# The differential loop: value products in two halves, and part of the join on GpSimd

## The chip, the cores and the metric

The program runs on one core of a Trainium2 chip. The time is the device time of one execution in microseconds (us). Three timed runs of the kernel before gave 3054.6 us as the median (3054.22 to 3056.43).

## The reference, cut to what matters

The whole program is a two-layer transformer block followed by a second two-layer block (the lines `for l in range(L)` of the second half). The change lies in one branch of the second block, the differential attention, which is computed once in each of its two layers:

```python
def diff_attend(q1, q2, k1, k2, v, lam):
    s1 = jnp.einsum('bqhd,bkhd->bhqk', q1, k1) * scale
    s2 = jnp.einsum('bqhd,bkhd->bhqk', q2, k2) * scale
    p = jax.nn.softmax(s1, axis=-1) - lam * jax.nn.softmax(s2, axis=-1)
    return jnp.einsum('bhqk,bkhd->bqhd', p, v)
```

There are 4 heads, 512 latent queries and 256 context queries. A latent query sees 768 keys (512 latent, then 256 context). A context query sees the 256 context keys and is computed in layer 0 only. After it, `diff_post` normalizes each head's 64 values and scales them.

## The kernel before, in words

Every engine has its own program, written out in order by hand (`block.tensor`, `block.vector`, `block.scalar`, `block.gpsimd`, `block.sync`). They meet in semaphores: `done(key)` marks a step, `after(key)` waits for it.

A *unit* is 128 queries of one head. `df_units(l)` lists them: for each pair of heads `j` 8 latent units (`"d"`, 4 query blocks by 2 heads), and in layer 0 then 4 context units (`"dc"`). That is 24 units in layer 0 and 16 in layer 1, 32 of them latent. The loop makes one turn `i` per unit, and each engine does in turn `i`:

- TensorE: the first score of unit `i` (`df_score`, half 0, two matmuls into a pair of PSUM banks), the transposes of the joined weights of unit `i-2` (`turn_wide`, six of 128x128; `DF_LAG` is 2), the second score of unit `i`. In every second turn it then does the value products of a pair of units, the two heads (`values`, 12 matmuls in the program, 24 in the trace), and at a head pair's end a broadcast of the row sums (`shares`).
- VectorE: the row maximum of the first score (`df_top`, line 2990), the join of unit `i-1` (`df_join`: a reciprocal on line 2996, a 128x1 product that is the factor, and a 768-column `p = q * factor + p`), the row maximum of the second score.
- ScalarE: exp of the first score, the copy of the transposed weights of unit `i-2` out of PSUM (`df_down`), exp of the second score. An exp with a row sum is an ACTIVATE and an ACTIVATION_READ_ACCUMULATOR.
- GpSimd: nothing in the loop.

What holds the turns together are rings. `PB` is six PSUM banks, taken in pairs for the scores and the transposes, or singly. `PO` is two more banks for the value sums. `PR` has four slots for the exp results, two per unit, so the first exp of unit `i+2` waits until the transposes of unit `i` have read their slot. `PT` has three slots for transposed weights, and `ST` six for the factors.

At fixed turns (`df_post_at`) the loop also normalizes the finished outputs of a head pair. ScalarE squares them, TensorE averages them into a bank (`df_norm`, a bank of `PB`), ScalarE takes a root from it (`df_root`), VectorE refines it (`df_post`, which frees the bank, then `df_gain`). Behind the loop stands the last group of the output projection, which needs the last normalized outputs (`branch_low`).

In the names of the rows below, `banks` is PSUM, `arena` the working memory, `block_tokens_low` and `block_tokens_high` hold the keys and queries of the differential loop, and `mats` the identity that transposes. Line 850 is the helper of every matmul, 851 of every transpose, 1670 of every ScalarE activation and 2348 of every VectorE scalar_tensor_tensor.

Of the kernel before, what the change touches and what calls it, by code (L numbers as in the profile page):

```python
# [31 lines left out]
P = 128  # L32
D = 1024
KD = D // P
T = 512
TB = T // P
# [250 lines left out]
def build(nc, A, known):  # L287

    ctx = ExitStack()
    with ctx:  # L290
# [359 lines left out]
        for l in range(L):  # L650
# [36 lines left out]
            b["STAGE"] = [nc.dram_tensor(f"df_stage{l}_{j}", (4, P, T + CT), F32, kind="Internal").ap() for j in range(2)]  # L687
            b["KS"], b["QS"] = [[S[:, 4 * j:4 * j + 4, :] for j in range(2)] for S in (com["HT"], HI)]
# [39 lines left out]
        def df_post_at(l):  # L728

            n = len(df_units(l))  # L730
            return {(0, 0): n // 2 + (2 if l == 0 else 5), (0, 1): n // 2 + 5, (1, 0): n if l == 0 else None}
# [59 lines left out]
        def _(eng):  # L791
# [158 lines left out]
            def values(us, S, V, blocks, okey, first, last, q):  # L950

                if first:
                    PO.take(okey)
                    if PO.former:
                        eng.wait_ge(*after(PO.former))
                o = PO.get(okey)
                for u in us:
                    for part in range(0, blocks, 4) if u[0] not in ("d", "dc") else (0,):
                        eng.wait_ge(*after(("pt", u, part)))
# [5 lines left out]
                i.then_inc(*done(*[turned(S, u).free(u) for u in us], *((("out", okey),) if last else ())))  # L965
# [377 lines left out]
            for l in range(L):  # L1343
# [210 lines left out]
                def df_norm(j, side):  # L1554
                    norm_sums((("od", "odc")[side], l, j), S, range(1), 1, "head64", (T, CT)[side], PB)
# [10 lines left out]
                out_proj(1, range(2 - both, KD))  # L1566
                us = df_units(l)
                for i in range(len(us) + DF_LAG + 1):
# [11 lines left out]
                    if DF_LAG < i and us[i - DF_LAG - 1][4] == 1:  # L1580
                        u = us[i - DF_LAG - 1]
                        values([u[:4] + (h,) for h in range(2)], S,
                               lambda u, c: S["V"][:, c + (TB if u[0] == "dc" else 0), 64 * (2 * u[2] + u[4]):64 * (2 * u[2] + u[4]) + 64],
                               6 if u[0] == "d" else 2, df_okey(u), u[3] == 0, df_ends(u), u[3])
                        if df_ends(u):
                            shares(df_okey(u), S, u[3] + 1, 2)
# [80 lines left out]
        def _(eng):  # L1667
# [364 lines left out]
            for l in range(L):  # L2032
# [213 lines left out]
                def df_root(j, i):  # L2246
                    root((("od", "odc")[i], l, j), S, PB, (T, CT)[i])
# [11 lines left out]
                for i in range(len(us) + DF_LAG + 1):  # L2259
# [18 lines left out]
                    if DF_LAG < i and df_ends(us[i - DF_LAG - 1]):  # L2278
                        u = us[i - DF_LAG - 1]
# [65 lines left out]
        def _(eng):  # L2345
# [434 lines left out]
            for l in range(L):  # L2780
# [211 lines left out]
                def df_join(u):  # L2992
# [5 lines left out]
                    stt(s[:, 4:5], s[:, 3:4], S["RS"].get(df_okey(u))[:, at:at + 1], LAM[l][:, 4:5], MUL, MUL).then_inc(*done())  # L2998
                    eng.wait_ge(vector_step, done.count)
                    p, q = S["PR"].get((u, 0))[:, 0:n], S["PR"].get((u, 1))[:, 0:n]  # L3000
                    stt(p, q, s[:, 4:5], p, MUL, ADD).then_inc(*done(("p", u), S["ST"].free(u), S["PR"].free((u, 1))))

                def df_post(j, i):
# [6 lines left out]
                    stt(n, PB.get(("ms", tag))[:, 0:(T, CT)[i]], EPS, n, ADD, MUL).then_inc(*done(PB.free(("ms", tag)), ("stepped", tag)))  # L3010
# [23 lines left out]
                for i in range(len(us) + DF_LAG + 2):  # L3034
# [18 lines left out]
                    if DF_LAG + 1 < i and df_ends(us[i - DF_LAG - 2]):  # L3053
# [287 lines left out]
```

## Time and profile before

| | |
|---|---|
| median of three runs | 3054.6 us |
| the profiled execution's own time | 3056.31 us |
| its span | 3054.5 us |
| TensorE busy | 2844.1 us (93%) |
| VectorE busy | 1419.5 us (46%) |
| ScalarE busy | 1126.6 us (37%) |
| GpSimd busy | 237.3 us (8%) |
| differential loop of layer 0 | about 1646 to 1742 us of the span |
| differential loop of layer 1 | about 2583 to 2654 us of the span |

Busy shares are averages over the whole program, and the loop is about 5% of it. What bounds the loop is read from its own stretch. In a row of the timeline the first number is the start in us from the span's start, the second the time from the start of the first to the end of the last instruction of the row, and what stands in brackets is how long the engine was idle before it and what ended the idle time. The granted TensorE clock is given as a share of full speed.

### The profile page before, as it was taken

Reading aid. Unit: us, or ns where it says so; the run is one execution under the profiler, and the core shown is the slowest. Engines: PE = TensorE matmul, PEld = TensorE weight load, DVE = VectorE, ACT = ScalarE, POOL = GpSimd, SP = SyncE. Lnnn points to the kernel's source line nnn. Section 1 sums busy time; section 2 is a strip of 40 time slices with the busy share of each in tenths; the row PEclk is TensorE's granted clock in tenths of the full one; section 3 lists DMA queues with packets and bytes.
Section 4 is the critical chain, followed back from the end, with each engine's and each line's share of the span. In section 5 each row is a group of like instructions: output and inputs, shape, how many; then the busy total and the mean of one; then the engine's idle time right before and its main releaser. Section 6 shows DMA issues by size and latency. Waiting matters only on the chain.

```text
span 3054.5 us, 40084 instructions
## 1 busy us (share of the span) xinstructions
PE 2844.1 (93%) x16210; PEld 2104.2 (69%) x16210; DVE 1419.5 (46%) x2142; ACT 1126.6 (37%) x1913; POOL 237.3 (8%) x230
## 2 busy tenths in 40 slices
PE   7999979989999799999998789999999999689998
PEld 5657845447668655457787578888888787578886
DVE  6665432246665522245436653333235544643444
ACT  4665421134654411143244542222222432543332
POOL 1011010000111200010011010000002011000001
PEclk9999989999999899999999789999999999899999
DMA  4012249971012379964426112332221234222220
GB/s 154 29 42 73 95 192 419 415 308 63 15 42 100 123 329 416 418 263 154 150 75 166 42 42 111 123 126 111 111 83 44 91 101 140 68 74 98 98 98 33
DMA packets 68198, 430.37 MB, mean 141 GB/s; under 512 B 8001, under 2 KB 8385, under 8 KB 20401
## 3 DMA queue, kind: packets, MB, share of 16 engines
q1 hardware_dynamic: 62432, 410.05, 35.2%
q0 software_dynamic: 4432, 15.67, 1.6%
q8 instruction: 131, 2.15, 0.3%
q10 hardware_dynamic: 1152, 2.10, 0.2%
q14 instruction: 51, 0.41, 0.0%
HBM read 418.87 MB, written 8.91 MB: 140 GB/s over the span
## 4 chain that ended last, share of the span: by engine, by line
PE 80%; DVE 7%; DMA 5%; ACT 4%; issue 2%; POOL 2%; SPq 0%; DVEq 0%; ACTq 0%; POOLq 0%
PE banks L850 76%; PE banks L851 3%; DMA weight<-in_w_up 3%; ACT arena L1670 3%; DVE arena L2348 3%; POOL arena L3145 1%; DVE arena L2990 1%; DVE weight_part L2452 1%; DMA weight<-in_w_in 1%; DMA weight<-in_ada_w 1%; ACT weight_part L1670 0%; DVE arena L2637 0%; DMA block_tokens_high<-df_stage 0%; DVE arena L2635 0%; DMA arena<-na_stage 0%
## 5 line engine op out<-in xcount | busy, mean ns | idle before, releaser
L1670 ACT ACTIVATE arena<-banks 128x512 f32<-128x512 f32 (+3 forms) x506 | 277.6, 551 | 892.0 <-PE banks L850 788.5
L850 PE MATMUL banks<-weight,arena 128*64 128x512 f32 (+4 forms) x2136 | 443.0, 581 | 21.4 <-DMA weight<-in_w_up 9.3
L850 PE MATMUL banks<-hidden,weight_part 128*128 128x512 f32 (+1 forms) x2304 | 446.8, 355 | 0.0
L850 PEld LDWEIGHTS banks<-hidden,weight_part 128*128 128x128 f32 x2304 | 381.1, 189 | 70.4 <-issue 3.8
L850 PE MATMUL banks<-tokens_high,weight_part 128*128 128x512 f32 (+1 forms) x1536 | 412.7, 360 | 8.7 <-ACT tokens_high L1670 5.5
L2452 DVE TENSOR_TENSOR weight_part<-weight,weight_part 128x2048 fp32r<-128x2048 f32 x124 | 285.8, 2308 | 191.6 <-ACT weight_part L1670 191.5
L1670 ACT ACTIVATE weight_part<-weight 128x2048 fp32r<-128x2048 f32 x124 | 236.4, 1908 | 372.9 <-PE banks L850 344.9
L850 PEld LDWEIGHTS banks<-weight,arena 128*64 128x64 f32 (+2 forms) x2136 | 150.8, 136 | 268.0 <-issue 246.3
L850 PEld LDWEIGHTS banks<-tokens_high,weight_part 128*128 128x128 f32 x1536 | 276.3, 192 | 62.8 <-DVE arena L2348 12.1
L3145 POOL TENSOR_TENSOR arena<-arena 128x512 f32<-128x512 f32 (+1 forms) x90 | 117.1, 1301 | 1999.1 <-ACT arena L1670 1732.3
L850 PE MATMUL banks<-tokens_low,weight_part 128*128 128x512 f32 (+1 forms) x768 | 265.4, 355 | 0.0
L850 PE MATMUL banks<-arena 128*64 128x128 f32 (+3 forms) x2048 | 223.7, 315 | 12.4 <-DMA arena<-na_stage 5.3
L2348 DVE SCALAR_TENSOR_TENSOR x<-banks,arena,x 128x512 f32<-128x512 f32 x192 | 142.4, 749 | 183.4 <-PE banks L850 182.7
L1670 ACT ACTIVATE arena<-banks,arena 128x512 f32<-128x512 f32 (+2 forms) x264 | 182.1, 694 | 90.7 <-DVE arena L2990 57.0
L851 PE MATMUL banks<-mats,arena 128*128 128x128 f32 (+1 forms) x1112 | 171.6, 289 | 39.4 <-DVE arena L2640 20.6
L3095 DVE TENSOR_TENSOR hidden<-arena,hidden 128x768 fp32r<-128x768 f32 (+1 forms) x64 | 52.8, 826 | 315.4 <-ACT hidden L1670 315.4
L851 PEld LDWEIGHTS banks<-mats,arena 128*128 128x128 f32 (+1 forms) x1112 | 131.6, 147 | 93.9 <-issue 45.0
L850 PEld LDWEIGHTS banks<-arena 128*64 128x64 f32 (+2 forms) x2048 | 148.2, 153 | 61.4 <-issue 41.5
L850 PE MATMUL banks<-block_tokens_high,weight_part 128*128 128x512 f32 (+1 forms) x640 | 165.1, 353 | 2.6 <-ACT block_tokens_high L1670 2.6
L2348 DVE SCALAR_TENSOR_TENSOR arena<-arena 128x256 f32<-128x256 f32 (+5 forms) x225 | 120.1, 545 | 97.9 <-ACT arena L1670 91.5
L2399 DVE TENSOR_REDUCE arena<-banks 128x1 f32<-128x512 f32 (+1 forms) x160 | 97.8, 634 | 131.7 <-PE banks L850 129.3
L850 PEld LDWEIGHTS banks<-tokens_low,weight_part 128*128 128x128 f32 x768 | 144.9, 190 | 20.4
(214 smaller groups left out, 3889.6 us busy)
## 6 DMA issues: line engine op xcount, KB each, us to landing
weight<-in_w_gate SPq DMA_DIRECT2D x64, 1024.0 KB, 13.6
weight<-in_w_up SPq DMA_DIRECT2D x64, 1024.0 KB, 8.0
weight<-in_w_down SPq DMA_DIRECT2D x64, 1024.0 KB, 11.1
weight<-in_w_ff SPq DMA_DIRECT2D x64, 1024.0 KB, 4.8
weight<-in_ada_w SPq DMA_DIRECT2D x48, 1024.0 KB, 6.3
weight<-in_w_in SPq DMA_DIRECT2D x28, 1024.0 KB, 5.3
weight<-in_w_o SPq DMA_DIRECT2D x8, 1024.0 KB, 4.8
weight<-in_w_mem_kv SPq DMA_DIRECT2D x8, 1024.0 KB, 5.0
```

The source lines that it names most:

```text
L850: mm = lambda o, a, b, first=True, last=True: eng.matmul(o, a, b, start=first, stop=last, skip_group_check=True)
L851: tr = lambda o, a, rows=P: eng.transpose(o, a, mat("ident", rows, rows))
L1670: act = lambda o, i, f=ACT.Copy, **k: eng.activation(o, i, f, **k)
L2348: stt = lambda o, a, s, b, p, q: eng.scalar_tensor_tensor(out=o, in0=a, scalar=s, in1=b, op0=p, op1=q)
L2399: eng.tensor_reduce(s[:, 0:1], PB.get(("S", u))[:, 0:n], AX, MAX, negate=True).then_inc(*done(("nb", u)))
L2452: tt(low, raw_of(key), high, SUB).then_inc(*done(("split", key)))
L2990: eng.tensor_reduce(s[:, half:half + 1], PB.get_pair(key)[:, 0:T + CT if u[0] == "d" else CT], AX, MAX, negate=True).then_inc(*done(("nb", ...
L3095: tt(hid[:, 4 + m, 0:N], t[:, 0:N], hid[:, m, 0:N], SUB).then_inc(*done(("hid", l, s, m), S["RT"].free((l, s, m))))
L3145: eng.tensor_tensor(a, a, squares_of(tag, S).get((tag, k))[:, 0:n], ADD).then_inc(*done(squares_of(tag, S).free((tag, k)), *((("summed", t ...
```

## The change

It does four things.

1. The value products of a latent pair of units are issued in two halves of three key blocks each. The first half stands where all of it stood (behind the second score of turn `i`), the second half in the next turn between the first score and the transposes. The broadcast of the row sums moves with the second half. Context units keep theirs in one piece.
2. The join of a latent unit is split by columns. VectorE does columns 0 to 511, and GpSimd does the 256 context columns in two instructions: `q = q * factor` (a broadcast of one column), and `p = p + q`, which also waits for VectorE's part. The transposes wait for GpSimd's (`"pc"`).
3. In layer 1 the bank of the head average is taken from `PO` in place of `PB` (`MS`).
4. The normalization turns move: layer 0's first from turn 14 to 15 and its last from 24 to 25, layer 1's first from 13 to 14. The loops have one turn more.

```diff
+            b["MS"] = PB if l == 0 else PO
...
-            return {(0, 0): n // 2 + (2 if l == 0 else 5), (0, 1): n // 2 + 5, (1, 0): n if l == 0 else None}
+            return {(0, 0): n // 2 + (3 if l == 0 else 6), (0, 1): n // 2 + (5 if l == 0 else 6), (1, 0): n + 1 if l == 0 else None}
+
+        def df_ended(l, i):
+
+            us = df_units(l)
+            return [u for u in (us[n] for n in (i - DF_LAG - 1, i - DF_LAG - 2) if 0 <= n < len(us)) if df_ends(u) and us.index(u) == i - DF_LAG - (2 if u[0] == "d" else 1)]
...
-            def values(us, S, V, blocks, okey, first, last, q):
+            def values(us, S, V, blocks, okey, first, last, q, part=None):
+
+                cs = range(blocks) if part is None else part
...
-                for c in range(blocks):
+                for c in cs:
                     for h, u in enumerate(us):
                         i = mm(o[rows * h:rows * h + rows, q * P:(q + 1) * P], V(u, c), turned(S, u).get(u)[:, c, :], c == 0, c == blocks - 1)
...
                     if i < len(us):
                         df_score(us[i], 0)
+                    if DF_LAG + 1 < i and us[i - DF_LAG - 2][4] == 1 and us[i - DF_LAG - 2][0] == "d":
+                        df_values(us[i - DF_LAG - 2], range(3, 6))
                     if DF_LAG <= i < len(us) + DF_LAG:
                         u = us[i - DF_LAG]
-                        eng.wait_ge(*after(("p", u)))
+                        eng.wait_ge(*after(("pc" if u[0] == "d" else "p", u)))
                         turn_wide(u, (u, 0), S, 6 if u[0] == "d" else 2)
                     if i < len(us):
                         df_score(us[i], 1)
-                    if DF_LAG < i and us[i - DF_LAG - 1][4] == 1:
+                    if DF_LAG < i <= len(us) + DF_LAG and us[i - DF_LAG - 1][4] == 1:
                         u = us[i - DF_LAG - 1]
...
+                        df_values(u, range(3 if u[0] == "d" else 2))
...
-                    stt(s[:, 4:5], s[:, 3:4], S["RS"].get(df_okey(u))[:, at:at + 1], LAM[l][:, 4:5], MUL, MUL).then_inc(*done())
+                    stt(s[:, 4:5], s[:, 3:4], S["RS"].get(df_okey(u))[:, at:at + 1], LAM[l][:, 4:5], MUL, MUL).then_inc(*done(("factor", u)))
                     eng.wait_ge(vector_step, done.count)
+                    n = T if u[0] == "d" else CT
...
-                    stt(p, q, s[:, 4:5], p, MUL, ADD).then_inc(*done(("p", u), S["ST"].free(u), S["PR"].free((u, 1))))
+                    stt(p, q, s[:, 4:5], p, MUL, ADD).then_inc(*done(("p", u), *((S["ST"].free(u), S["PR"].free((u, 1))) if u[0] == "dc" else ())))
...
+                for u in df_units(l):
+                    if u[0] == "d":
+                        p, q = S["PR"].get((u, 0))[:, T:T + CT], S["PR"].get((u, 1))[:, T:T + CT]
+                        eng.wait_ge(*after(("factor", u)))
+                        eng.tensor_tensor(q, q, S["ST"].get(u)[:, 4:5].broadcast_to([P, CT]), MUL).then_inc(*done())
+                        eng.wait_ge(pool_step, done.count)
+                        eng.wait_ge(*after(("p", u)))
+                        eng.tensor_tensor(p, p, q, ADD).then_inc(*done(("pc", u), S["ST"].free(u), S["PR"].free((u, 1))))
```

On TensorE, in two turns of layer 1 before (`banks_0` to `banks_2` are the three pairs of `PB`, `banks_3` is `PO`; the six transposes are `x6`, the value products `x12`):

```order
L851 MATMUL banks_0<-mats,arena 128x128 x6
L850 MATMUL banks_1<-block_tokens_low1,block_tokens_high 128x512
L850 MATMUL banks_1<-block_tokens_low1,block_tokens_high 128x256
L850 MATMUL banks_3<-arena 64x128 x12
L850 MATMUL banks_2<-block_tokens_low1,block_tokens_high 128x512
L850 MATMUL banks_2<-block_tokens_low1,block_tokens_high 128x256
L851 MATMUL banks_0<-mats,arena 128x128 x6
L850 MATMUL banks_1<-block_tokens_low1,block_tokens_high 128x512
```

The same place in the changed kernel:

```order
L857 MATMUL banks_2<-mats,arena 128x128 x6
L856 MATMUL banks_0<-block_tokens_low1,block_tokens_high 128x512
L856 MATMUL banks_0<-block_tokens_low1,block_tokens_high 128x256
L856 MATMUL banks_3<-arena 64x128 x6
L856 MATMUL banks_1<-block_tokens_low1,block_tokens_high 128x512
L856 MATMUL banks_1<-block_tokens_low1,block_tokens_high 128x256
L856 MATMUL banks_3<-arena 64x128 x6
L857 MATMUL banks_2<-mats,arena 128x128 x6
L856 MATMUL banks_0<-block_tokens_low1,block_tokens_high 128x512
```

Half of the value products has moved behind the next first score, and there it stands ahead of the transposes.

On TensorE at the head average in the middle of layer 1 before (`arena,mats` 128x512 is the average):

```order
L850 MATMUL banks_3<-arena 64x128 x12
L850 MATMUL banks_0<-arena,mats 128x512
L850 MATMUL banks_1<-block_tokens_low1,block_tokens_high 128x512
L850 MATMUL banks_1<-block_tokens_low1,block_tokens_high 128x256
L851 MATMUL banks_2<-mats,arena 128x128 x6
L850 MATMUL banks_0<-block_tokens_low1,block_tokens_high 128x512
```

And in the changed kernel:

```order
L856 MATMUL banks_3<-arena,mats 128x512
L856 MATMUL banks_2<-block_tokens_low1,block_tokens_high 128x512
L856 MATMUL banks_2<-block_tokens_low1,block_tokens_high 128x256
L857 MATMUL banks_0<-mats,arena 128x128 x6
L856 MATMUL banks_1<-block_tokens_low1,block_tokens_high 128x512
```

The average has left the pair `banks_0` that the second score of the same turn took behind it.

## Rows read from the trace of the kernel before

**Rows 1.** Both loops as windows: us; busy (x) by engine; clock, DMA share, GB/s.
```profile
1646.00:1742.00 96.00, 69.19 (x457) 50.68 (x458) 73.06 (x141) 62.12 (x135) 0.00 (x0) 0.81 0.27 78
2583.00:2654.00 71.00, 52.36 (x385) 39.23 (x383) 54.36 (x88) 47.51 (x87) 0.00 (x0) 0.83 0.39 121
```

**Rows 2.** Timeline of layer 1's loop, two turns at full clock.
```profile
2601.22 0.15 DVE L2996 RECIPROCAL arena<-arena 128x1 f32<-128x1 f32 x1
2601.41 1.27 DVE L2348 SCALAR_TENSOR_TENSOR arena<-arena 128x1 f32<-128x1 f32 x2
...
2602.23 0.80 ACT L1670 ACTIVATE arena<-banks 128x768 f32<-128x768 f32 x1
...
2603.18 0.85 PE L851 MATMUL banks<-mats,arena 128*128 128x128 f32 x6
2603.58 0.90 ACT L1670 ACTIVATE arena<-banks,arena 128x768 f32<-128x768 f32 x1 [0.55 <-DVE arena L2990]
...
2604.61 0.16 DVE L2996 RECIPROCAL arena<-arena 128x1 f32<-128x1 f32 x1 [0.19 <-ACT arena L1670]
...
2605.23 1.53 PE L850 MATMUL banks<-arena 128*64 128x128 f32 x24
...
2607.41 0.96 DVE L2990 TENSOR_REDUCE arena<-banks 128x1 f32<-128x768 f32 x1 [0.47 <-PE banks L850]
...
2608.29 0.15 DVE L2996 RECIPROCAL arena<-arena 128x1 f32<-128x1 f32 x1
```

**Rows 3.** VectorE by shape, layer 0's loop: count | busy, mean ns | idle before.
```profile
L2348 DVE SCALAR_TENSOR_TENSOR arena<-arena 128x768 f32<-128x768 f32 x16 | 16.3, 1019 | 0.6
L2348 DVE SCALAR_TENSOR_TENSOR arena<-arena 128x256 f32<-128x256 f32 x11 | 5.2, 473 | 0.3
L2348 DVE SCALAR_TENSOR_TENSOR arena<-arena 128x512 f32<-128x512 f32 x4 | 2.8, 703 | 0.7 <-ACT arena L1670 0.7
```

**Rows 4.** Timeline of layer 1's loop, its start at the low clock.
```profile
2594.69 1.48 PE L851 MATMUL banks<-mats,arena 128*128 128x128 f32 x6
...
2596.22 0.16 DVE L2996 RECIPROCAL arena<-arena 128x1 f32<-128x1 f32 x1 [0.19 <-ACT arena L1670]
...
2597.24 2.52 PE L850 MATMUL banks<-arena 128*64 128x128 f32 x24
```

**Rows 5.** Timeline of layer 1's loop, around the head average.
```profile
2627.16 0.15 DVE L2996 RECIPROCAL arena<-arena 128x1 f32<-128x1 f32 x1
...
2635.64 0.94 PE L850 MATMUL banks<-block_tokens_low,block_tokens_high 128*128 128x512 f32 x4 [3.22 <-issue]
...
2647.44 0.16 DVE L2996 RECIPROCAL arena<-arena 128x1 f32<-128x1 f32 x1 [0.46 <-ACT arena L1670]
```

**Rows 6.** Timeline of the tails of layer 0's and layer 1's loops.
```profile
1737.73 1.90 ACT L1670 ACTIVATE weight_part<-weight 128x2048 fp32r<-128x2048 f32 x1
...
2648.97 0.87 PE L851 MATMUL banks<-mats,arena 128*128 128x128 f32 x6 [1.06 <-DVE arena L2348]
```

**Rows 7.** GpSimd, 256 columns: the timeline behind layer 0's loop.
```profile
1766.02 1.52 POOL L3145 TENSOR_TENSOR arena<-arena 128x256 f32<-128x256 f32 x2 [0.16 <-POOL arena L3145]
```

**Rows 8.** GpSimd, 256 columns: its group by shape over the whole span.
```profile
L3145 POOL TENSOR_TENSOR arena<-arena 128x256 f32<-128x256 f32 x24 | 26.3, 1096 | 98.3 <-ACT arena L1670 96.8 <-POOL arena L3145 0.2
```

**Rows 9.** Timeline ahead of layer 0's loop: GpSimd and VectorE side by side.
```profile
1612.72 1.84 POOL L3252 TENSOR_TENSOR df_QL<-arena,df_QH 128x768 fp32r<-128x768 f32 x1
...
1630.94 0.69 DVE L2972 TENSOR_TENSOR arena<-arena 128x512 f32<-128x512 f32 x1
...
1631.10 2.23 POOL L3252 TENSOR_TENSOR df_QL<-arena,df_QH 128x768 fp32r<-128x768 f32 x1
...
1632.33 1.55 DVE L2980 TENSOR_TENSOR df_KL<-arena,df_KH 128x512 fp32r<-128x512 f32 x1 [0.24 <-ACT df_KH L1670]
```

**Rows 10.** Timeline: GpSimd starting on a VectorE result.
```profile
1609.60 0.69 DVE L2972 TENSOR_TENSOR arena<-arena 128x512 f32<-128x512 f32 x1
...
1610.46 1.29 POOL L3135 TENSOR_TENSOR arena<-arena 128x512 f32<-128x512 f32 x1 [11.49 <-DVE arena L2972]
```

More of the change, by code:

```diff
@@ L957, in values @@
                 for u in us:
-                    for part in range(0, blocks, 4) if u[0] not in ("d", "dc") else (0,):
-                        eng.wait_ge(*after(("pt", u, part)))
+                    for piece in range(0, blocks, 4) if u[0] not in ("d", "dc") else (0,):
+                        eng.wait_ge(*after(("pt", u, piece)))
                 n = len(us)
                 rows = P // n
-                for c in range(blocks):
+                for c in cs:
                     for h, u in enumerate(us):
                         i = mm(o[rows * h:rows * h + rows, q * P:(q + 1) * P], V(u, c), turned(S, u).get(u)[:, c, :], c == 0, c == blocks - 1)
-                i.then_inc(*done(*[turned(S, u).free(u) for u in us], *((("out", okey),) if last else ())))
+                if blocks - 1 in cs:
+                    i.then_inc(*done(*[turned(S, u).free(u) for u in us], *((("out", okey),) if last else ())))
             def take_bank(key):
@@ L1566, in _, with df_values @@
                 out_proj(1, range(2 - both, KD))
+                def df_values(u, part):
+                    blocks = 6 if u[0] == "d" else 2
+                    values([u[:4] + (h,) for h in range(2)], S,
+                           lambda u, c: S["V"][:, c + (TB if u[0] == "dc" else 0), 64 * (2 * u[2] + u[4]):64 * (2 * u[2] + u[4]) + 64],
+                           blocks, df_okey(u), u[3] == 0, df_ends(u), u[3], part)
+                    if df_ends(u) and blocks - 1 in part:
+                        shares(df_okey(u), S, u[3] + 1, 2)
                 us = df_units(l)
-                for i in range(len(us) + DF_LAG + 1):
+                for i in range(len(us) + DF_LAG + 2):
                     for (j, side), n in df_post_at(l).items():
@@ L2258, in _ @@
                 us = df_units(l)
-                for i in range(len(us) + DF_LAG + 1):
+                for i in range(len(us) + DF_LAG + 2):
                     if i == df_post_at(l)[0, 1] + 2:
@@ L2277, in _ @@
                         df_exp(us[i], 1)
-                    if DF_LAG < i and df_ends(us[i - DF_LAG - 1]):
-                        u = us[i - DF_LAG - 1]
+                    for u in df_ended(l, i):
                         shares(df_okey(u), S, u[3] + 1)
@@ L3033, in _ @@
                 us = df_units(l)
-                for i in range(len(us) + DF_LAG + 2):
+                for i in range(len(us) + DF_LAG + 3):
                     if i == df_post_at(l)[0, 1] + 3:
@@ L3052, in _ @@
                         df_top(us[i], 1)
-                    if DF_LAG + 1 < i and df_ends(us[i - DF_LAG - 2]):
-                        u = us[i - DF_LAG - 2]
+                    for u in df_ended(l, i - 1):
                         c = int(u[0] == "dc")
```

13 lines of the change are left out of this document (4 added, 9 removed).

## The prediction

> **What bounds it now.** I first read the two loops as windows [rows 1]: in layer 0 VectorE is busy 73 of 96 us, in layer 1 54 of 71, more than any other engine, at a mean TensorE clock of 0.81 and 0.83. TensorE, 93% busy over the program, is idle here for 27 and 19 us. Whatever is won in these 167 us is won outright, since the projection behind the loop waits for its outputs. Outside them the change touches nothing but the order in which single banks are taken. Then I followed the timeline from one reciprocal of the join to the next, which is one turn.
>
> Two kinds of turn stand in [rows 2]. A turn without value products takes 2604.61 - 2601.22 = 3.39 us, and the chain is closed inside it. Reciprocal 0.19 with its gap, factor and join 1.27 (the join is 1.02 of it [rows 3]), the maximum 0.90 until exp starts at 2603.58, exp with its row sum 1.03 until the next reciprocal: 3.39. A turn with value products takes 2608.29 - 2604.61 = 3.68. There the chain runs over TensorE: second score, 24 matmuls in 1.53, next first score, and VectorE had been idle for 0.47 when its maximum could start. So a pair costs 7.07 at full clock.
>
> At the low of the two clock levels (1.2 GHz; the transposes take 1.48 in place of 0.85 [rows 2, 4]) the short turns are 3.4 too, and the first value turn 2601.22 - 2596.22 = 5.00, since its products take 2.52 [rows 4].
>
> In the middle of layer 1 four turns take 2647.44 - 2627.16 = 20.3 us [rows 5]. The largest piece is the bank of the head average. The second score of that turn takes the same pair and waits until VectorE has read the average in its refinement, behind ScalarE's root; TensorE sits idle for 3.22 us and comes back at the low clock.
>
> **The change, part by part.**
>
> *Join, VectorE.* 768 columns take 1.02, 256 take 0.47, 512 take 0.70 [rows 3]. The line through 256 and 768 gives 0.75 for 512; I take that, because the join's scalar is a pointer as in those two. It saves 0.27 per latent unit, with 0.32 as the other bound. The vector lap becomes 3.12. 32 x 0.27 = 8.6 us would be the gain if this lap bounded everywhere.
>
> *Join, GpSimd.* Two instructions of 256 columns per unit. Undisturbed such an add takes 0.73 [rows 7]; the mean of all 24 is 1.10, disturbed ones included [rows 8]. A multiply by a broadcast column does not appear in the trace; I bound it by these two and take 0.73, the nearer in operation. The question is what happens beside VectorE. In [rows 9] the same 768-column subtraction takes 1.84 alone and 2.23 when a VectorE instruction with two SBUF inputs had started 0.16 us ahead of it; and a VectorE one that normally takes 0.69 takes 1.55 when it starts during GpSimd's, ending 0.55 after GpSimd's end at 1633.33. So whoever starts second waits for the first. Who is first here? GpSimd starts 1610.46 - 1610.29 = 0.17 after a VectorE result [rows 10], while VectorE follows its own in about 0.03. So VectorE's 512 columns go first, GpSimd's multiply is held until they end, and runs for another 0.58 (0.73 less about 0.14 of its start-up, which the wait covers: 1.84 + 0.53 - 2.23 in rows 9). The add follows after 0.06 and meets only VectorE maxima, which read PSUM. Counted from the reciprocal, the factor is ready at 0.42, VectorE's part at 1.2, GpSimd's at 1.2 + 0.58 + 0.06 + 0.73 = 2.6. Before, the whole join was ready at 1.45.
>
> The Trainium skill, "SBUF — State Buffer", "Who interferes with whom", says that a VectorE instruction with two SBUF inputs and a GpSimd instruction that reads SBUF exclude each other for the whole instruction, and that the order of issue decides who is blocked. By that rule, the trace agrees, with the 2.23 and the 1.55. "GPSIMD Engine Reference", "Engine selection", advises against two-input elementwise work there as about twice as slow; 0.73 against 0.47 here is 1.55 times.
>
> *What the later transposes cost.* The transposes of unit i free the slot for the first exp of unit i+2. That lap is now 2.65 (transposes start) + 0.85 + 0.90 (exp) + 0.80 (copy down) + 1.00 (second exp with its row sum) + 0.05 = 6.25 [rows 2] for two units, just the 2 x 3.12 of the vector lap. So at full clock GpSimd's detour hides with nothing to spare. At the low clock the transposes add 0.63: 6.9 for two units against 6.8 before.
>
> *Value halves.* In a value turn TensorE now does transposes (until 0.35 after exp has ended), second score, half of the products (0.77), first score, ready at 2.5; with the maximum 0.96 the turn is 3.46. The other half falls in the next turn ahead of the transposes, which wait for GpSimd then anyway. A pair is 3.46 + 3.12 = 6.58, against 7.07: 0.49 less. If GpSimd's part were free it would be 6.24.
>
> *Bank.* In layer 1 the average leaves the pair ring, and the 3.22 us wait goes. What is next: VectorE's refinement stands in the turn all the same (two passes of 0.70 each, and two more a turn later [rows 3]), and GpSimd's held multiply then slips in ahead of them, 0.6 each time. I work the four turns out as 3.3, 3.3, 5.1 and 5.2, so 16.9 in place of 20.3: 3.4 less. Of PO's two banks the one taken was freed turns before, so no wait takes its place. Layer 0 keeps its bank and its stalls.
>
> *Tails.* Layer 1's last transposes, which started as soon as VectorE's join ended (the row at 2648.97), start about 1.2 later, behind ScalarE's weight rounding; 1.0 of it reaches the end. In layer 0 the last average moves a turn, behind the 1.90 us weight rounding on ScalarE [rows 6] that it used to precede; I take 1.4 later (bounds 0 and 1.9).
>
> *Sum.* Layer 1: low-clock turns +0.1; first value turn -0.8 (half of 2.52 goes, 0.5 comes back by the later transposes); three pairs at full clock -0.5, -0.5 and -0.25 (the third also carries the broadcast of the row sums, which delays the transposes now); the middle -3.4; tail +1.0: -4.35. Layer 0: low-clock turns +0.1; three value turns -0.5 each; one at the low clock -1.3; four short turns -0.27 each, -1.1; GpSimd ahead of the refinement twice, +1.2; tail +1.4: -1.2. Together -5.55, rounded -5.6. The profiled execution took 3056.3 us, 1.7 above the median; 3056.3 - 5.6 = 3050.7, and against the median 3054.6 - 5.6 = 3049.0.
>
> **Rivals.**
>
> A, slower: VectorE is held. If GpSimd's multiply gets the read path first, the 512-column join waits some 0.58 in each latent unit, as the 1.55 did. The vector lap is then 3.39 - 0.27 + 0.58 = 3.70, 0.31 more than before in the 20 turns or so that are short, +6.2, and nothing is won in value turns. With the middle at -1.5 and the tails +2.4 that is +7: 3061.7. It decides as soon as GpSimd starts before VectorE does. Against it: 0.17 against 0.03.
>
> B, no gain or slower: the slot lap bounds. If the broadcast multiply takes 1.10 instead of 0.73, the lap is 6.6 to 7.0, a pair at full clock about 7.0, and low-clock pairs 7.3 against 6.8. Then what the turns gave outside the middle (-5.95 in the sum) becomes +0.8, the middle keeps -2.5, tails and held refinements +3.6: +1.9, so 3056.5, and 3 or 4 more if the multiply takes longer yet. For it: no slack in my lap. Against it: GpSimd's 0.73 is steady where VectorE is away.
>
> C, only the bank counts in full: the middle -3.4, half of the -5.95, tails and held refinements +3.6: -2.8, so 3051.8. For it: the tails are certain, the turns' gain rests on laps that are level.
>
> D, the clock: TensorE has less idle time, stays at its full level through the middle and into the projection behind, where matmuls now run slow after waits. Ten us of work at the low level take 10 x 0.85 / 1.48 = 5.7 at the high one [rows 2, 4]; 4.3 less than the forecast is 3044.7. Against it: the loops already have 0.8 of full speed.
>
> **Chances.** The forecast 0.40, A 0.10, B 0.18, C 0.14, D 0.18. A measurement here tells 0.2%, about 6 us, from no change. The forecast lies just within that line, so I split it: 0.23 faster, 0.17 the same. Faster: 0.23 and D, 0.41. Slower: A and 0.07 of B, its upper end, 0.17. The same: 0.17, C, and 0.11 of B, 0.42. The range from 3042.5 to 3058.5 takes in D and B's middle and leaves out A and B's upper end; the forecast's own range is 3046 to 3052.
>
> **What would show it.** GpSimd's multiply at 1.3 to 1.5 us in the profile (held), its add at 0.73; VectorE's join at 0.70 to 0.75. Pairs of turns at full clock at 6.6 us. No idle time over 1 us on TensorE at the head average of layer 1, and still about 2.5 in layer 0. Layer 0's last root later by more than a microsecond against the end of its loop. Wrong would be: joins of 1.3 us (A), turns that end in waits of ScalarE for transposes (B), or a loop in layer 1 that is shorter by less than 2 us.

## The result: slower by about 0.4%

The changed kernel took 3072.8 us (median of 5 runs, 3065.2 to 3073.6) beside 3055.4 for the kernel before; the ratio is 1.0047 with a 95% interval of [1.0037, 1.0058]. Measured again later, it was 1.0036 [1.0023, 1.0050]. The forecast was 3049.0 with a range up to 3058.5: wrong in sign. What happened is rival A's mechanism, to which I had given one chance in ten, and two costs besides that no case had at their size: a wait for a bank in the turn of the row sums, and longer tails.

The profiled execution took 3065.2 (span 3063.4), 8.9 us of span more than before. It was the fastest of the five; the rest of the difference lies in other executions, whose mean granted clock is 0.964 to 0.968 in place of its 0.970. So the profile can account for about half of the 17 us; for the rest I compare whole runs below.

The two loops as windows, columns as in [rows 1]:

```profile
1645.00:1742.00 97.00, 67.11 (x452) 47.02 (x451) 76.00 (x140) 60.59 (x132) 22.17 (x32) 0.83 0.25 69
2585.00:2656.00 71.00, 52.60 (x355) 36.85 (x353) 58.98 (x89) 45.01 (x85) 21.35 (x31) 0.88 0.41 119
```

VectorE should have had less to do and has more: 76.0 against 73.1 us in layer 0, 59.0 against 54.4 in layer 1. GpSimd, idle before, works 22 and 21 us. To put the 8.9 us in their places I measure each loop from the first reciprocal of its joins to the last. First the changed kernel, then the kernel before (its last one is in [rows 5]):

```profile
1648.44 0.16 DVE L3009 RECIPROCAL arena<-arena 128x1 f32<-128x1 f32 x1 [0.21 <-ACT arena L1684]
...
1738.76 0.16 DVE L3009 RECIPROCAL arena<-arena 128x1 f32<-128x1 f32 x1 [0.63 <-ACT arena L1684]
...
2591.88 0.16 DVE L3009 RECIPROCAL arena<-arena 128x1 f32<-128x1 f32 x1 [0.21 <-ACT arena L1684]
...
2654.48 0.16 DVE L3009 RECIPROCAL arena<-arena 128x1 f32<-128x1 f32 x1 [1.06 <-ACT arena L1684]
```

```profile
1649.06 0.16 DVE L2996 RECIPROCAL arena<-arena 128x1 f32<-128x1 f32 x1 [0.21 <-ACT arena L1670]
...
1737.26 0.16 DVE L2996 RECIPROCAL arena<-arena 128x1 f32<-128x1 f32 x1
...
2586.02 0.16 DVE L2996 RECIPROCAL arena<-arena 128x1 f32<-128x1 f32 x1 [0.21 <-ACT arena L1670]
```

The five stretches add up to 8.9 (before rounding): ahead of the loops -0.6, layer 0's loop +2.1 (88.2 to 90.3), from it to layer 1's loop +4.4, layer 1's loop +1.2 (61.4 to 62.6), and the rest +1.9.

**One turn at full clock** (it answers to [rows 2]):

```profile
2606.28 0.16 DVE L3009 RECIPROCAL arena<-arena 128x1 f32<-128x1 f32 x1 [0.19 <-ACT arena L1684]
...
2606.48 1.46 DVE L2361 SCALAR_TENSOR_TENSOR arena<-arena 128x1 f32<-128x1 f32 x2
2606.78 0.61 POOL L3270 TENSOR_TENSOR arena<-arena 128x256 f32<-128x256 f32 x1 [1.55 <-DVE arena L2361]
...
2608.08 0.72 POOL L3273 TENSOR_TENSOR arena<-arena 128x256 f32<-128x256 f32 x1 [0.69 <-DVE arena L2361]
...
2608.86 0.88 PE L857 MATMUL banks<-mats,arena 128*128 128x128 f32 x6 [0.69 <-POOL arena L3273]
...
2609.87 0.16 DVE L3009 RECIPROCAL arena<-arena 128x1 f32<-128x1 f32 x1 [0.19 <-ACT arena L1684]
```

The row of 1.46 is the factor and the join, one by one:

```profile
2606.48 0.22 DVE L2361 SCALAR_TENSOR_TENSOR arena<-arena 128x1 f32<-128x1 f32 x1
```

```profile
2606.74 1.20 DVE L2361 SCALAR_TENSOR_TENSOR arena<-arena 128x512 f32<-128x512 f32 x1
```

VectorE's join starts 0.04 after the factor's end and GpSimd's multiply 0.08 after it, in all 32 units of the trace. The multiply runs its 0.61 undisturbed; factor and join on VectorE take 1.46, where 768 columns had taken 1.27. They end at 2607.94, 0.55 after the multiply. The turn lasts 3.59, and nearly every turn at full clock does, with value products (3.68 before) or without (3.39). A pair went from 7.07 to 7.17. The turn is built as before, 0.20 + 1.46 + 0.90 + 1.03: the reciprocal with its gap, factor and join, the maximum, the exp.

**A new wait.** In layer 1 one turn takes 8.00, where the same turn took 3.84 before:

```profile
2628.44 1.04 PE L856 MATMUL banks<-mats,arena 128*64 128x128 f32 x16
2628.65 0.15 DVE L3009 RECIPROCAL arena<-arena 128x1 f32<-128x1 f32 x1
...
2634.03 0.59 ACT L1684 ACTIVATE arena<-banks 128x512 f32<-128x512 f32 x1
...
2634.71 0.96 PE L856 MATMUL banks<-block_tokens_low,block_tokens_high 128*128 128x512 f32 x2 [2.61 <-issue]
...
2635.47 1.48 PE L857 MATMUL banks<-mats,arena 128*128 128x128 f32 x6
...
2636.65 0.15 DVE L3009 RECIPROCAL arena<-arena 128x1 f32<-128x1 f32 x1
```

The 16 matmuls are the broadcast of the row sums (`shares`). Before they stood behind the second score; with the second half of the products they have come between first score and transposes, and take a bank of the ring of pairs there. The next first score needs that bank and starts at 2634.71, right behind ScalarE's copy out of it, which itself stands behind an exp. TensorE then runs at its low level (transposes 1.48). Layer 0 has the same wait in a turn of 6.37 (2.78 before), still at full clock until the wait:

```profile
1685.20 0.59 ACT L1684 ACTIVATE arena<-banks 128x512 f32<-128x512 f32 x1
1685.88 0.98 PE L856 MATMUL banks<-block_tokens_low,block_tokens_high 128*128 128x512 f32 x2 [1.65 <-ACT arena L1684]
```

**Tails.** Layer 0, the changed kernel and then the kernel before:

```profile
1739.10 1.91 ACT L1684 ACTIVATE weight_part<-weight 128x2048 fp32r<-128x2048 f32 x1
...
1741.17 0.64 ACT L1684 ACTIVATE arena<-arena 128x512 f32<-128x512 f32 x1
...
1741.86 2.08 PE L856 MATMUL banks<-arena,mats 128*128 128x512 f32 x2 [1.55 <-ACT arena L1684]
...
1751.55 0.77 PE L856 MATMUL banks<-branch_high,weight_part 128*128 128x512 f32 x1 [4.59 <-DVE branch_low L2842]
```

```profile
1737.88 1.12 PE L850 MATMUL banks<-arena,mats 128*128 128x512 f32 x2 [2.18 <-ACT arena L1670]
...
1746.53 0.76 PE L850 MATMUL banks<-branch_high,weight_part 128*128 128x512 f32 x1 [2.68 <-DVE branch_low L2829]
```

The squares (0.64) stand behind the weight rounding, as foreseen, and the average itself takes 2.08 instead of 1.12: it runs at TensorE's low level, behind waits of 1.65 and 1.55 (before it had waited 2.18 and ran at full clock); from the last reciprocal to the output product it is 12.8 us against 9.3. Layer 1, in the same order:

```profile
2656.28 1.11 POOL L3273 TENSOR_TENSOR arena<-arena 128x256 f32<-128x256 f32 x1 [0.69 <-DVE arena L2431]
2657.44 0.87 PE L857 MATMUL banks<-mats,arena 128*128 128x128 f32 x6 [1.58 <-POOL arena L3273]
...
2659.37 2.82 PE L856 MATMUL banks<-arena 128*64 128x128 f32 x24 [1.05 <-ACT arena L1684]
...
2663.86 0.69 DVE L2441 TENSOR_TENSOR arena<-banks,arena 128x512 f32<-128x512 f32 x1 [7.05 <-ACT arena L1684]
```

```profile
2650.89 1.53 PE L850 MATMUL banks<-arena 128*64 128x128 f32 x24 [1.05 <-ACT arena L1670]
...
2654.09 0.69 DVE L2428 TENSOR_TENSOR arena<-banks,arena 128x512 f32<-128x512 f32 x1 [5.07 <-ACT arena L1670]
```

Last reciprocal to scaled output: 9.4 against 6.65. The last value products run at the low level (2.82 against 1.53). TensorE's order is the same as before at this place; what differs ahead of them is the idle time, 1.58 before the last transposes against 1.06. GpSimd's add takes 1.11 beside a VectorE subtraction.

### The profile page after: what moved, and what is told of

It is laid out like the page before. It is cut to its first block, busy times and chain, and to the rows that moved or that the text cites. A ratio compares the mean times of both kernels' runs of the same rounds, so it can differ in the third digit from the quotient of the medians.

```text
span 3063.4 us, 40197 instructions
## 1 busy us (share of the span) xinstructions
PE 2844.2 (93%) x16210; PEld 2102.0 (69%) x16210; DVE 1426.9 (47%) x2142; ACT 1128.0 (37%) x1913; POOL 282.3 (9%) x294
## 4 chain that ended last, share of the span: by engine, by line
PE 79%; DVE 8%; DMA 5%; ACT 4%; issue 2%; POOL 2%; SPq 0%; DVEq 0%; ACTq 0%; POOLq 0%
PE banks L856 75%; PE banks L857 4%; DVE arena L2361 3%; ACT arena L1684 3%; DMA weight<-in_w_up 3%; POOL arena L3158 1%; DVE weight_part L2465 1%; DVE arena L3003 1%; DMA weight<-in_w_in 1%; ACT weight_part L1684 0%; DVE arena L2650 0%; DMA weight<-in_ada_w 0%; DMA arena<-na_stage 0%; DVE arena L2648 0%; DVE x L2361 0%
## 5 line engine op out<-in xcount | busy, mean ns | idle before, releaser
L856 PE MATMUL banks<-arena 128*64 128x128 f32 (+3 forms) x2048 | 226.1, 315 | 12.3 <-DMA arena<-na_stage 5.4
L2361 DVE SCALAR_TENSOR_TENSOR arena<-arena 128x512 f32<-128x512 f32 (+4 forms) x225 | 127.1, 576 | 101.1 <-ACT arena L1684 94.6
```

Source lines behind the costliest of these rows:

```text
L856: mm = lambda o, a, b, first=True, last=True: eng.matmul(o, a, b, start=first, stop=last, skip_group_check=True)
L2361: stt = lambda o, a, s, b, p, q: eng.scalar_tensor_tensor(out=o, in0=a, scalar=s, in1=b, op0=p, op1=q)
```

## Experiments

They ran in three groups, each on a chip of its own beside the kernel before: e1, e2, e3, e5 (its median there 3057.2); the changed kernel again, e6, e8, e9 (3056.8); e7, e10, e11, e12 (3056.6). Across groups only the ratios to it are compared. "Loops" are first to last reciprocal of layer 0 and layer 1 in the profiled execution, read as above; those of the kernel before are from the profile above. The ratios are of the runs of one group and aren't exactly the ratios of the medians.

| kernel | median us | ratio [95%] | loops us |
|---|---|---|---|
| before | 3056.8 | 1 | 88.2, 61.4 |
| changed, again | 3067.4 | 1.0036 [1.0023, 1.0050] | 91.6, 61.4 |
| e1 join whole on VectorE | 3052.9 | 0.9992 [0.9982, 1.0002] | 84.7, 61.3 |
| e2 split join alone | 3060.6 | 1.0010 [0.9998, 1.0022] | 90.7, 63.4 |
| e3 GpSimd second | 3059.8 | 1.0008 [0.9998, 1.0018] | 86.3, 58.6 |
| e5 bank alone | 3056.7 | 0.9999 [0.9991, 1.0008] | 87.0, 59.9 |
| e6 e1, row sums last | 3054.2 | 0.9995 [0.9984, 1.0006] | 86.5, 57.3 |
| e7 e6, average earlier | 3052.7 | 0.9991 [0.9981, 1.0002] | 82.1, 55.2 |
| e8 halves not at ends | 3050.9 | 0.9982 [0.9970, 0.9994] | 87.8, 57.5 |
| e9 e8, GpSimd second | 3050.0 | 0.9981 [0.9971, 0.9991] | 87.3, 55.4 |
| e10 e9, 128 columns | 3050.3 | 0.9983 [0.9973, 0.9992] | 86.4, 56.1 |
| e11 changed, 128 columns | 3063.1 | 1.0025 [1.0014, 1.0035] | 87.0, 60.4 |
| e12 e8, bank in both layers | 3045.9 | 0.9968 [0.9958, 0.9979] | 79.5, 55.4 |

**The changed kernel again.** No edit.

> The changed kernel itself once more, beside the others on one chip. Theory H (held joins, 32 x 0.18, and tails later by 3.5 and 2.7): its profile shows turns of 3.58 again and the time is 9 or more above the kernel before on this chip, ratio 1.003 or more. Rival N (the 17 us of the first measurement were mostly a matter of TensorE's clock in those executions): ratio 1.001 or less, with the same turns.

Turns of 3.57 to 3.59 again, and 10.6 us above before, outside N: H. The loss is real. By its median it is smaller than the first 17, but the two intervals overlap. The turn with the broadcast took 6.95 here, behind the same 2.61 of idle time.

**e1_join_on_vector.** The changed kernel without GpSimd's part (its loop is gone as well):

```
-                    n = T if u[0] == "d" else CT
                     p, q = S["PR"].get((u, 0))[:, 0:n], S["PR"].get((u, 1))[:, 0:n]
...
-                        eng.wait_ge(*after(("pc" if u[0] == "d" else "p", u)))
+                        eng.wait_ge(*after(("p", u)))
...
```

> The changed kernel, with the whole join of 768 columns back on VectorE and nothing of it on GpSimd; value halves, bank and turns of the average stay. Theory H (GpSimd's multiply holds VectorE's join on the shared read path): a turn at full clock falls from the 3.58 of the changed kernel to about 3.4 (reciprocal with its gap 0.19, factor and join 1.27, maximum 0.90, exp 1.03), in value turns too, since the second half of the products no longer stands there; 32 x 0.18 = 5.8, and each tail gets back about 1, so some 7 to 8 less than the changed kernel's 3072.8: 3065. Rival S (what costs is the bank of the row sums in the middle of the turn and the later average, which stay here): at most 2 less, 3071, with the turns of 8.0 us in layer 1 and 6.4 us in layer 0 still there.

Turns at full clock are 3.39 to 3.40, value turns too, and the ratio is 0.9992 against the changed kernel's 1.0036, some 13 us less. H, and by more than its price of 7 to 8. The turn with the broadcast is still 7.5 and layer 1's tail still 8.4 us, so those two don't come from GpSimd alone.

**e2_gpsimd_join_alone.** The kernel before with the split join only (the last hunk of the diff, the two of `df_join`, and the wait of the transposes).

> The kernel before, with the split join alone: VectorE joins 512 columns, GpSimd multiplies and adds the other 256, the transposes wait for GpSimd. Value products whole, banks and turns as before. Theory H: turns without value products go from 3.39 to about 3.6, turns with them from 3.68 to 3.7 or more since they run over TensorE anyway and the transposes come later; about 16 x 0.2 + 16 x 0.1 = 4.8, and 1 per tail: 3055.4 + 7 = 3062. Rival S: the join in two parts is neutral in the loops, only the tails pay: 3057.

3.57 in short turns, 3.67 to 3.69 in value turns, loops longer by 2.5 and 2.0. The time says 1.0010, just not told from 1. H's mechanism, half its price (3.4 us by the medians, where it had 7).

**e3_gpsimd_second.** The decisive one: the changed kernel with

```
-                        eng.wait_ge(*after(("factor", u)))
+                        eng.wait_ge(*after(("p", u)))
                         eng.tensor_tensor(q, q, S["ST"].get(u)[:, 4:5].broadcast_to([P, CT]), MUL).then_inc(*done())
                         eng.wait_ge(pool_step, done.count)
-                        eng.wait_ge(*after(("p", u)))
```

> The changed kernel, with GpSimd's multiply waiting for the end of VectorE's part of the join in place of the factor: the order that the prediction had assumed, now forced. Theory H: VectorE's factor and join fall from 1.46 to about 0.98; GpSimd's part is ready 1.2 + 0.05 + 0.61 + 0.06 + 0.73 = 2.65 after the reciprocal. If the slot lap of 6.25 for two turns is right, turns at full clock go from 3.58 to about 3.3: 32 x 0.28 = 9, 3064. Rival L (the lap through GpSimd bounds, whoever is first): the transposes come 0.2 later than now, a pair stays at 7.1 or more and the time is 3072 or above.

One turn of its timeline:

```profile
2605.75 0.15 DVE L3009 RECIPROCAL arena<-arena 128x1 f32<-128x1 f32 x1
...
2605.94 1.01 DVE L2361 SCALAR_TENSOR_TENSOR arena<-arena 128x1 f32<-128x1 f32 x2
...
2607.03 0.61 POOL L3270 TENSOR_TENSOR arena<-arena 128x256 f32<-128x256 f32 x1 [2.08 <-DVE arena L2361]
...
2607.72 0.73 POOL L3272 TENSOR_TENSOR arena<-arena 128x256 f32<-128x256 f32 x1
...
2608.50 0.88 PE L857 MATMUL banks<-mats,arena 128*128 128x128 f32 x6
...
2608.87 0.16 DVE L3009 RECIPROCAL arena<-arena 128x1 f32<-128x1 f32 x1
```

The turn is 3.12, GpSimd's part is ready 2.70 after the reciprocal, and pairs at full clock come to 6.3 to 6.6: my 3.12, 2.6 and 6.58, once the order I had assumed is forced. By the ratios it is worth 0.0028 of the time, some 8.6 us (1.0036 less 1.0008, the two intervals together give about 0.0017 either way).

But e1, with no GpSimd in the join, stands beside it in the same group at 3052.9 against 3059.8, 0.0016 lower, give or take 0.0014. So even in the order that I had assumed, nothing shows that the split join is worth its place.

**e11_first_128.** The changed kernel with the border between the engines moved, multiply still on the factor:

```
-                    n = T if u[0] == "d" else CT
+                    n = T + P if u[0] == "d" else CT
...
-                        p, q = S["PR"].get((u, 0))[:, T:T + CT], S["PR"].get((u, 1))[:, T:T + CT]
+                        p, q = S["PR"].get((u, 0))[:, T + P:T + CT], S["PR"].get((u, 1))[:, T + P:T + CT]
...
-                        eng.tensor_tensor(q, q, S["ST"].get(u)[:, 4:5].broadcast_to([P, CT]), MUL).then_inc(*done())
+                        eng.tensor_tensor(q, q, S["ST"].get(u)[:, 4:5].broadcast_to([P, CT - P]), MUL).then_inc(*done())
```

> The changed kernel, with 640 columns of the join on VectorE and 128 on GpSimd, whose multiply still starts on the factor. Theory H (VectorE is held until GpSimd's multiply ends, so by the multiply's length less its start-up): the multiply of 128 columns should take 0.35 to 0.4 where 256 take 0.61, the hold 0.2 to 0.25 where it was 0.47; factor and join 1.14 + 0.23 = 1.37, turn 3.50 in place of 3.58; 8 x 0.32 us less of held time in all and GpSimd ready 0.5 earlier: 3064 where the changed kernel stands at 3067.4. Rival F (a fixed loss of 0.47 whenever both start together): factor and join 1.6, turn 3.72, 3070 or more.

Joins by shape in layer 1's loop, the count, the busy time and the mean ns of one: in e11, then in e10, where GpSimd comes second, then the changed kernel's 512 columns (16 joins and 3 other instructions) and e3's.

```profile
L2361 DVE SCALAR_TENSOR_TENSOR arena<-arena 128x640 f32<-128x640 f32 x16 | 18.0, 1124 | 0.6
...
L3270 POOL TENSOR_TENSOR arena<-arena 128x128 f32<-128x128 f32 x16 | 6.4, 399 | 47.1 <-DVE arena L2361 47.1
```

```profile
L2356 DVE SCALAR_TENSOR_TENSOR arena<-arena 128x640 f32<-128x640 f32 x16 | 14.2, 884 | 0.6
```

```profile
L2361 DVE SCALAR_TENSOR_TENSOR arena<-arena 128x512 f32<-128x512 f32 x19 | 21.6, 1143 | 0.6
...
L3270 POOL TENSOR_TENSOR arena<-arena 128x256 f32<-128x256 f32 x16 | 9.8, 614 | 43.5 <-DVE arena L2361 43.5
```

```profile
L2361 DVE SCALAR_TENSOR_TENSOR arena<-arena 128x512 f32<-128x512 f32 x19 | 14.2, 757 | 0.6
```

A multiply of 0.40 holds VectorE for 1.124 - 0.884 = 0.24, one of 0.61 for (1143 - 757) x 19 / 16 = 0.46: each time GpSimd's duration less 0.15 or 0.16. Turns are 3.50. That is H as priced, and excludes a fixed loss of 0.47. The ratio, 0.0011 or 3 us below the changed kernel's, fits but isn't told apart from it by itself.

**e5_bank_alone.** The kernel before with layer 1's average in the other ring, in three places like

```
-                    root((("od", "odc")[i], l, j), S, PB, (T, CT)[i])
+                    root((("od", "odc")[i], l, j), S, PO if l else PB, (T, CT)[i])
```

> The kernel before, with layer 1's head average in the ring of two single banks and nothing else. By the prediction's step on the bank the 3.22 us of idle TensorE in the middle of layer 1's loop go and 3.4 us come out of its four turns: 3052. Rival G (given back: VectorE's refinement and gain stand in the same turns and the loop waits for them instead): within 1 of the time before, 3054.5 to 3055.5.

Layer 1's last four turns took 4.09 + 4.71 + 5.77 + 3.38 = 17.95 instead of 20.28: 2.3 less, not 3.4. The whole run shows nothing, as G had it, though its interval (-2.7 to +2.4 us) doesn't exclude 2.3.

**e6_vector_shares_last.** e1, with the broadcast back at the end of TensorE's turn:

```
-                    if df_ends(u) and blocks - 1 in part:
-                        shares(df_okey(u), S, u[3] + 1, 2)
...
+                    for u in df_ended(l, i):
+                        shares(df_okey(u), S, u[3] + 1, 2)
```

> As e1_join_on_vector (whole join on VectorE), and TensorE's broadcast of the row sums at the end of its turn, behind the second score and the value products, as in the kernel before; in the changed kernel it stands between first score and transposes, takes a bank of the pair ring there, and the next first score waits for ScalarE's copy. Theory R (the order of the ring makes the turns of 7.5 us in layer 1 and 6.4 us in layer 0): they fall to about 4 and 3.4 and three other turns with broadcasts by less; 5 to 6 less than e1: 3047. Rival G (the wait is only moved: ScalarE's copy still comes after exp, and the first score of the turn after needs the same bank): within 1.5 of e1's 3052.9.

```profile
2630.98 1.09 PE L856 MATMUL banks<-mats,arena 128*64 128x128 f32 x16 [0.79 <-DVE arena L2361]
2632.01 0.61 PE L856 MATMUL banks<-block_tokens_low,block_tokens_high 128*128 128x512 f32 x2
```

The next first score follows the broadcast without idle time, and layer 1's turn is 4.1 where e1's was 7.5: R is shown for that turn. The runs don't confirm a gain (0.9995 against 0.9992, intervals overlapping), so what the turn gives is under what they can tell. The turn of layer 0 is 6.35 here too, but at the low clock (granted 0.50 from 1680 to 1690 us) and without the wait. In e7, whose code is the same up to there, it is 4.15 at full clock, as R had it: in the changed kernel and in e1 that turn, too, is made by the ring.

**e7_average_earlier.** e6 with `(1, 0): n` for `n + 1` in `df_post_at`.

> As e6_vector_shares_last (whole join on VectorE, broadcast of the row sums at the end of the turn), and layer 0's last average of latents a turn earlier again, where the kernel before has it: its squares and root stand ahead of ScalarE's weight rounding. Theory T (that move is the larger part of layer 0's tail, 12.8 us from the last reciprocal to the first product of the output's low half in the changed kernel against 9.3 before): 1.9 or more comes back, e6's 3054.2 becomes 3052. Rival: the scaled output itself is a turn later by the halves, the squares wait for it, and nothing comes back: 3054.

T isn't borne out. From the last reciprocal to the output product it is 13.2 us here against e6's 12.3; the squares do stand ahead of the weight rounding again, but the average runs at the low level (2.08, in e6 1.13). From layer 0's loop to layer 1's it is 851.8 us against e6's 852.7, and the ratio is 0.0004 lower, not told apart.

**e8_whole_at_ends.** e5, and value halves except where a pair of heads ends; everything else stands at the turns of before:

```
+                    if DF_LAG + 1 < i and us[i - DF_LAG - 2][4] == 1 and us[i - DF_LAG - 2][0] == "d" and not df_ends(us[i - DF_LAG - 2]):
+                        df_values(us[i - DF_LAG - 2], range(3, 6))
...
+                        df_values(u, range(2 if u[0] == "dc" else 6 if df_ends(u) else 3))
```

> The kernel before with the bank of e5_bank_alone, and value products in two halves only in turns in which no pair of heads ends; the last products of each pair of heads stay whole, so the row sums, outputs, averages and tails stand at the turns of before. Join whole on VectorE. Theory: halves are worth 0.29 in each such value turn at full clock (3.68 to 3.39) and 1 or more at the low clock, 5 to 6 turns in each loop; loops of 85 and 58 us in place of 88 and 61, tail of layer 1 at 6.65 from the last reciprocal to the scaled output as before: 3057 - 6 = 3051. Rival: halves at ends are what matters, or the clock takes it back: 3056 to 3057.

3050.9 as expected, and faster than before beyond the interval. Value turns are 3.39 to 3.40 at full clock, and the tail of layer 1 is 6.65 again. The loops were 87.8 and 57.5, where 85 and 58 had been expected: in this profile layer 0 gave almost nothing, since two of its turns took 4.42 and 4.84 at the low clock, so the time fits better than its working.

**e9_ends_gpsimd_second.** e8 with e3's join.

> As e8_whole_at_ends, with the join split as in e3_gpsimd_second (GpSimd's multiply waits for VectorE's 512 columns). e3's turns at full clock were 3.12 to 3.57 where e1's were 3.40 throughout, so by those rows the loops gain 1 us each at most and the tails lose 1 each: the same as e8 within 2. Rival L (the lap through GpSimd's 2.65 bounds and TensorE idles ahead of every group of transposes, which lowers its clock): 4 or more above e8.

The same as e8, so the split join gives nothing here either. It differs from e3 only in what the halves at the ends bring with them (row sums in the middle of the turn, outputs and averages a turn later, tails): 0.9981 against 1.0008, so that costs 0.0027, about 8 us, give or take 4.

**e10_second_128.** e9 with e11's border.

> As e9_ends_gpsimd_second, with 640 columns of the join on VectorE and 128 on GpSimd, whose multiply waits for VectorE. By the laps: VectorE's factor and join 1.01 + 0.13 = 1.14, turn at full clock 3.26; GpSimd ready at about 2.3 after the reciprocal in place of 2.7, slot lap 5.95 for two turns against 6.52, so that VectorE's lap bounds with slack: turns of 3.26 throughout at full clock where e9 has 3.12 to 3.52, TensorE less idle ahead of its transposes. Loops 1 to 2 us shorter each than e9: 3047. Rival (VectorE's lap does not decide there, 256 columns were as good): 3050 within 1.5.

Most turns at full clock are 3.25 to 3.33 as worked out, though some are 3.5, and the time is e9's. Beyond that point VectorE's lap in full-clock turns decides nothing that whole runs show.

**e12_both_layers_po.** e8 with the averages of both layers in the ring of single banks (`PO` for `PO if l else PB`).

> As e8_whole_at_ends, with the averages in the ring of two single banks in layer 0 too. By e5's rows (layer 1's middle lost 2.3 us of its 20.3 by this bank) the two turns of 6.8 and 5 us in layer 0's loop should become about 5 and 4.5: 2 to 3 us less, 3048. Rival: in layer 0 four outputs share those two banks, the average waits for one of them to be read, and the stall stays or grows: 3051 to 3055.

```profile
1650.00:1734.00 84.00, 62.53 (x443) 44.10 (x442) 70.53 (x139) 58.55 (x131) 0.00 (x0) 0.88 0.27 72
...
2580.00:2640.00 60.00, 44.31 (x340) 30.94 (x340) 53.55 (x88) 45.87 (x85) 0.00 (x0) 0.94 0.39 110
```

The fastest: 3045.9, 0.9968 [0.9958, 0.9979], and below the changed kernel by 0.7%. Beside e8, which differs in layer 0's bank alone, it is 0.0014 lower, give or take 0.0016: likely, not certain. The turns fit: those around layer 0's average take 4.4 us less than e8's (17.3 for 21.7), e8's stall of 2.59 behind the average is gone, and the average itself starts without a wait. In layer 0 the turns around the average, 4.84, 6.90, 4.96 and 6.44 before, are 3.40, 4.72, 4.97 and 4.22, and the clock over the loops is 0.88 and 0.94 where [rows 1] has 0.81 and 0.83.

## Why the prediction was wrong

*The step that failed* is "So VectorE's 512 columns go first, GpSimd's multiply is held until they end", and with it the rule it came from, "whoever starts second waits for the first". I had set GpSimd's 0.17 after a VectorE result [rows 10] against VectorE's own 0.03. The order of the starts came out as I had said: VectorE's join starts 0.04 after the factor, GpSimd's multiply 0.08. Yet the multiply runs its 0.61 and VectorE, 0.04 ahead by its record, is the one held, in all 32 units. So the order of starts in the records doesn't tell who waits when they lie this close; what does, no run shows. Nor was 0.17 a typical start: in e3, behind the join of 512 columns, the multiply starts after 0.08 as well. The hold is 0.46 per unit, not rival A's 0.58, so the turn is 3.58 and not 3.70: over 32 units 32 x 0.46 = 15 us of held VectorE, of which e3 gives back 8.6. The whole term of 8.6 hung on a margin of 0.14; 1 in 10 for A was far too little.

*The join's saving and laps* were right as sizes of a turn: 0.757 for 512 columns against my 0.75, 3.12 in e3, pairs of 6.3 to 6.6 against 6.58. As a gain of the whole kernel the saving isn't seen even with the order forced: e3 is no faster than e1, and e9 is the same as e8.

*The multiply*, 0.61, was below my 0.73; rival B's condition of 1.10 didn't come about.

*Value halves* work: value turns lose their extra 0.29 in e1 and e8 at full clock. But I priced them as if only the split products moved. At the end of a pair of heads the row sums, the output and the average move with them. The sum gave the broadcast of the row sums only a later start of the transposes (the third pair's -0.25 in place of -0.5) and the turn behind that pair nothing at all. There the next first score waits for the bank of the broadcast, and the turn went from 3.84 to 8.00; in layer 0 the like turn went from 2.78 to 6.37. e9 against e3 puts all that moves at the ends at about 8 us.

*The bank*: no stall of 3.22 is left, as said; the last four turns take 17.8 in the changed kernel (2636.65 to 2654.48), against my 16.9, and e5's profile puts the bank's own share at 2.3 in place of 3.4.

*Tails*: +1.0 and +1.4 were +2.7 and +3.5 (12.8 less 9.3). For GpSimd's share in layer 1 the +1.0 was near: e9 has 7.9 from the last reciprocal to the scaled output where e8 has 6.65. What the halves and the clock add there had no term: e1, without GpSimd, has 8.4, and its last products take 2.83 for 1.53, 1.3 of its 1.7. In layer 0 nothing of the 3.5 is GpSimd's, since e1 has 12.8 too, and about 1.0 is the average at the low level (e8, with its ends in place and that average at 2.07, has 10.2); 2.5 remain for the moved ends, where I had 1.4 and at most 1.9.

*Sum*: the forecast of -5.6, 8.6 for the failed step and 8 for the ends give +11, and the second measurement gave +10.6. That is no confirmation, since 8.6 and 8 are the differences between the changed kernel, e3 and e9, and add up by construction. What can be compared is e9, which has neither cost: it measured 5.8 us less than before by its ratio, near the forecast. That is in part luck. e8 reaches the same without the split join, to which the forecast owed part of its turns' gain. In rivals B and C the gain of the turns outside the middle was put at -5.95; the terms of the sum give -5.75, which moves C's time by 0.1.

*What stays open*: why VectorE is the one held; why the first measurement showed 17 and the second 10.6 us; and how much of the ends' 8 us is each of their three parts, since the steps of e6 and e7 were too small for the runs to tell.

## What to carry to other kernels

Where two engines start on one result and hold each other up, don't derive who waits from starts that lie a tenth of a microsecond apart: force the order with a wait, price both orders, and measure beside them the kernel that leaves the second engine out. When half of an operation moves a turn later, list what hangs on its end (outputs, sums, banks of a ring) and follow each, and keep the operation whole at those ends. The bank for the slow reader was the smallest part of this change. In layer 1 alone no gain shows in whole runs (0.9999); in both layers, with the halves that keep their ends, it makes the fastest kernel here, though not one that is certainly faster than e8.

## What was not expected of the hardware

VectorE is held even when its record starts first. In e11:

```profile
2599.73 1.13 DVE L2361 SCALAR_TENSOR_TENSOR arena<-arena 128x640 f32<-128x640 f32 x1
2599.77 0.40 POOL L3270 TENSOR_TENSOR arena<-arena 128x128 f32<-128x128 f32 x1 [1.83 <-DVE arena L2361]
```

The join of 640 columns takes 1.13 here and 0.88 undisturbed, though it starts 0.04 ahead of the multiply. The Trainium skill, "SBUF — State Buffer", "Who interferes with whom", lets the order of issue decide who is blocked; the starts in the records, 0.04 apart, do not show that order.

The same code ran at different clock levels in two executions. These are the same 12 value matmuls in layer 0's loop, in e6 and in e7, whose code is the same up to there:

```profile
1685.69 1.55 PE L856 MATMUL banks<-arena 128*64 128x128 f32 x12
```

```profile
1680.69 0.88 PE L856 MATMUL banks<-arena 128*64 128x128 f32 x12
```

Single runs of one kernel lie up to 17 us apart (3046.4 to 3062.9 for the kernel before in the second group), and the mean granted clock goes with the time (0.972 to 0.974 in the fastest four, 0.967 to 0.970 in the slowest four). So loops of one profile are compared turn by turn here, not by their sum.
